# Seven landing places for the down projection's units, and three small moves ahead of the first gate

## The reference, cut to what matters

```python
h = _rms(x, g_mix); z = h @ w_in
za, zu, zv, zq, zg = jnp.split(z, SPLITS, axis=-1)
ya = gelu(_s5(za, ...))                                  # diagonal state space model
ya = (ya * sigmoid(ya @ w_glu + b_glu)) @ w_a_out
yb = _sgu(zu, zv, ...) @ w_b_out                         # gelu(zu) * (w_s @ layernorm(gelu(zv)) + b_s)
yc = _mem_xattn(zq, mem, g_mem, w_kv) @ w_c_out          # 4 heads, 256 memory rows
gates = sigmoid(zg + b_gate)                             # three gates of 1024
x = x + (gates0 * ya + gates1 * yb + gates2 * yc) @ w_out
hf = _rms(x, g_ffn)
x = x + (silu(hf @ w_gate) * (hf @ w_up)) @ w_down       # hidden width 2816
return _rms(x, g_final)
```

## Time and profile before

| | |
|---|---|
| median of 3 runs | 777.63 us (777.61 to 778.03) |
| the profiled execution's own time | 777.84 us |
| its span, first to last instruction | 776.1 us |
| TensorE busy | 765.6 us, 99% |
| VectorE busy | 541.6 us, 70% |
| ScalarE busy | 354.3 us, 46% |
| POOL busy | 315.8 us, 41% |
| granted TensorE clock, mean | 0.999 |

### The profile page before, as it was taken

One profiled execution on the slowest core, in us unless ns is written; L12 is line 12 of the kernel. 1 busy time (PEld: TensorE's weight loads), 2 busy tenths in 40 slices (PEclk: granted clock), 3 DMA queues, 4 the chain that ended last, 5 costly groups with the idle time before them and its releaser, 6 DMA issues.

```text
span 776.1 us, 9751 instructions
## 1 busy us (share of the span) xinstructions
PE 765.6 (99%) x3576; PEld 630.8 (81%) x3576; DVE 541.6 (70%) x729; ACT 354.3 (46%) x526; POOL 315.8 (41%) x169
## 2 busy tenths in 40 slices
PE   9999999999999999999999999999999999999996
PEld 7778887788888888888888888888888888778885
DVE  6999997684848484345865677777776777635686
ACT  6896567644545434543433333332323233444463
POOL 4456646233333333444444344534444453920000
PEclk9999999999999999999999999999999999999999
DMA  7744332132222432232324465666756557677852
GB/s 274 297 142 135 110 109 86 31 102 82 82 82 82 132 139 82 82 108 84 106 96 146 147 206 180 214 230 203 228 186 196 204 200 246 196 246 249 280 179 109
DMA packets 39667, 121.98 MB, mean 157 GB/s; under 512 B 4048, under 2 KB 4176, under 8 KB 37840
## 3 DMA queue, kind: packets, MB, share of 16 engines
q1 hardware_dynamic: 39488, 121.26, 47.1%
q10 hardware_dynamic: 144, 0.26, 0.1%
HBM read 104.99 MB, written 16.52 MB: 157 GB/s over the span
## 4 chain that ended last, share of the span: by engine, by line
PE 78%; DVE 13%; ACT 3%; issue 2%; DMA 2%; POOL 1%; SPq 0%; POOLq 0%; DVEq 0%; ACTq 0%
PE bank L1557 21%; PE bank L1558 21%; PE bank L1559 21%; PE bank L1926 4%; PE bank L1928 4%; PE bank L1927 4%; DVE pow_tmp L969 3%; DVE tab_tmp L969 1%; DVE s5p L969 1%; PE bank L1798 1%; DMA xT<-xt_dram 1%; DMA raw<-mix_dram 1%; DVE m_lo L974 1%; ACT prob L655 1%; DVE h_lo L974 0%
## 5 line engine op out<-in xcount | busy, mean ns | idle before, releaser
L500 POOL TENSOR_TENSOR w_lo<-raw,w_hi 128x1024 fp32r<-128x1024 f32 x90 | 219.1, 2434 | 298.1 <-ACT w_hi L561 298.1
L561 ACT ACTIVATE w_hi<-raw 128x1024 fp32r<-128x1024 f32 x112 | 118.6, 1060 | 309.1 <-PE bank L1559 302.3
L1557 PE MATMUL bank<-h_hi,w_hi 128*128 128x512 f32 x608 | 238.2, 392 | 0.5 <-DVE th L969 0.4
L1559 PE MATMUL bank<-h_hi,w_lo 128*128 128x512 f32 x608 | 236.7, 389 | 0.0
L1558 PE MATMUL bank<-h_lo,w_hi 128*128 128x512 f32 x608 | 236.6, 389 | 0.0
L1557 PEld LDWEIGHTS bank<-h_hi,w_hi 128*128 128x128 f32 x608 | 114.1, 188 | 25.5 <-DVE th L969 1.3
L1559 PEld LDWEIGHTS bank<-h_hi,w_lo 128*128 128x128 f32 x608 | 114.1, 188 | 23.9
L1558 PEld LDWEIGHTS bank<-h_lo,w_hi 128*128 128x128 f32 x608 | 114.2, 188 | 23.3 <-issue 0.2
L505 POOL TENSOR_TENSOR w_lo<-raw,w_hi 128x512 fp32r<-128x512 f32 x48 | 67.2, 1422 | 56.3 <-ACT w_hi L561 49.7
L969 DVE TENSOR_TENSOR mix<-mix 128x512 f32<-128x512 f32 x44 | 47.2, 1072 | 10.5 <-DMA mix<-w_dram 9.4
L969 DVE TENSOR_TENSOR lo<-raw,hi 128x1536 fp32r<-128x1536 f32 (+1 forms) x19 | 33.3, 1757 | 28.8 <-ACT hi L888 28.8
(11 more groups left out here) (297 smaller groups left out, 1391.7 us busy)
## 6 DMA issues: line engine op xcount, KB each, us to landing
raw<-w_dram SPq DMA_DIRECT2D x112, 512.0 KB, 3.4
mix<-w_dram SPq DMA_DIRECT2D x11, 1024.0 KB, 7.7
mix_dram<-mix SPq DMA_DIRECT2D x11, 1024.0 KB, 6.4
raw<-w_dram SPq DMA_DIRECT2D x32, 256.0 KB, 3.9
raw<-mix_dram SPq DMA_DIRECT2D x28, 256.0 KB, 3.9
half_dram<-odd SPq DMA_DIRECT2D x11, 256.0 KB, 7.9
second<-half_dram SPq DMA_DIRECT2D x3, 768.0 KB, 6.0
raw<-mix_dram SPq DMA_DIRECT2D x3, 768.0 KB, 4.3
```

The lines of the kernel that those rows point to most:

```text
L500: nc.gpsimd.tensor_tensor(w_lo[:, s, :], raw[:, s, :], fv(w_hi[:, s, :]), ALU.subtract).then_inc(w_ready, 1)
L561: nc.scalar.activation(w_hi[:, slot, :], raw[:, slot, :], ACT.Copy).then_inc(w_rounded, 1)
L1557: mm(out, a[0], b[0], start=first, stop=False)
L1559: return mm(out, a[1], b[0], start=False, stop=last)
```

## The change: what it does

Four things. (1) The units get seven raw places instead of five, a third one behind the first two `raw_d` and one where `mix` had its second half; `UNIT_SLOT` and the waits of `load_unit` follow, unit 10 is loaded ahead of the first of three, and ScalarE's first rounding of three waits for one more split. (2) The first gate waits for three groups of the gating unit instead of four, and the gate in bank 1 for the fourth. (3) ScalarE rounds tile T_VU+6 ahead of the scaling of head 2. (4) VectorE makes the memory's diagonal ahead of the products with the state space model's input matrix.

```diff
-        raw_d = [at(f"raw_d{i}", o_h + 12288 + 4096 * i, [P, TILE]) for i in range(2)]
-        unit_raw = [raw[:, 0, :], raw[:, 1, :], raw_c[:, :], raw_d[0][:, :], raw_d[1][:, :]]
-        UNIT_SLOT = (0, 1, 2, 3, 4, 0, 1, 2, 0, 1, 2)
+        raw_d = [at(f"raw_d{i}", o_h + 12288 + 4096 * i, [P, TILE]) for i in range(3)]
+        raw_e = at("raw_e", o_e + 12288, [P, TILE])
+        unit_raw = [raw[:, 0, :], raw[:, 1, :], raw_c[:, :], *(r[:, :] for r in raw_d), raw_e[:, :]]
+        UNIT_SLOT = (0, 1, 2, 3, 4, 5, 6, 0, 1, 2, 6)
...
-        unit_loaded = [sem(f"unit_loaded{i}") for i in range(5)]
+        unit_loaded = [sem(f"unit_loaded{i}") for i in range(7)]
...
                 if k < 2:
                     sp.wait_ge(w_ready, T_DN - 1 + k)
-                elif 3 <= k < 5:
+                elif 3 <= k < 6:
                     sp.wait_ge(w_used, T_DN)
-                elif k >= 5:
-                    unit_split(sp, {5: 0, 6: 1, 7: 2, 8: 5, 9: 6, 10: 7}[k])
+                elif k == 6:
+                    sp.wait_ge(mix_stored, 16 * PAIRS)
+                elif k > 6:
+                    unit_split(sp, {7: 0, 8: 1, 9: 2, 10: 6}[k])
...
-            for k in range(6, 10):
+            for k in range(6, PAIRS):
                 load_unit(k)
             load_three(0)
-            load_unit(10)
             load_three(1)
...
             round_weights(T_VU + 5)
+            round_weights(T_VU + 6)
             softmax_scale(2)
             gelu_u(1)
-            round_weights(T_VU + 6)
             round_weights(T_VU + 7)
...
                 if u == 0:
-                    act.wait_ge(w_ready, T_DN + 5)
+                    act.wait_ge(w_ready, T_DN + 6)
...
                 low_tile(norms["m"], m_hi, m_lo, memf, C_GMEM, k)
 
+            token_scale(2, 2, mtstd[:, :], mtrstd[:, :], mdiag[:, :, :], diag_m)
+
             bre, bim, cre, cim = (grid(c0) for c0 in (C_BRE, C_BIM, C_CRE, C_CIM))
...
             link(tt(bpow[1][:, L - 1, :, :], bb_tmp[:, 2, :, :], bb_tmp[:, 3, :, :], ALU.add))
-            token_scale(2, 2, mtstd[:, :], mtrstd[:, :], mdiag[:, :, :], diag_m)
-
...
-            pe.wait_ge(sgu_taken, 4)
+            pe.wait_ge(sgu_taken, 3)
             pe.wait_ge(pt_act, 4)
...
                 def gate(j, b, free):
                     if free > 0:
                         pe.wait_ge(j1_g, free)
+                    elif b == 1:
+                        pe.wait_ge(sgu_taken, 4)
```

## The result

The changed kernel takes 779.4 us against 777.65 for the kernel before, measured beside it on the same chip. The ratio is 1.0025, with a 95% interval of 1.0017 to 1.0033. It is slower by a quarter of a per cent: less than 2 us, but the interval does not take in 1. The forecast was 777.8, and its range ended at 779.1. The profiled execution took 779.2 us, with a span of 777.5 where it was 776.1 before: +1.4. The medians in this document are of the undisturbed executions; the profiled one of the run that has the rounding alone was disturbed (959.48 us at a mean clock of 0.753), so no timeline of that kernel is read.

What follows compares the result with a forecast made beforehand. TensorE was taken as the bound, busy 765.6 of 776.1 us, so only waits could move. +1.9 up to the first gate and -1.7 for the places gave +0.2: 778.0 profiled, 777.8 as median; range 775.2 to 779.1.

Steps and rivals of the forecast that it cites:

- The diagonal: Memory's diagonal made earlier on VectorE: TensorE's wait at 47.38 goes, 0.42 to 0.5 gained, 0.2 carried to the scores at 102.
- The rounding's chain of collisions: Before the first gate: T_VU+6 rounded early makes POOL and VectorE meet twice on their port; value rows late, 2.4 lost.
- the second collision: POOL's whole-tile split of T_J1 against VectorE's short scaling and last two table sums: VectorE waits some 2.0.
- The values product itself: First values product on TensorE, waiting for the value rows: starts at 132.2 instead of 129.81, 2.4 lost.
- The gate: First gate, asking for three groups instead of four: TensorE's wait there goes, 0.5 gained once.
- Seven places: Down projection: units 7 to 10 load earlier, waits at units 9 and 10 go, 1.7 gained (late end 1.2).
- Rival 1: Before the first gate: the collisions don't come; 774.5, or 775.6 with the second collision alone; chance 0.19.
- Rival 2: Down projection: added loads delay units 3 and 4, costing 1.4 to 3.6, total 779.2 to 781.4; chance 0.10.
- POOL's backlog: Down projection, in rival 2: POOL's waiting work hides 0.8 of the delay of unit loads.

## Why the prediction was wrong, step by step

**The diagonal.** Right as to its wait: none stands at its product. The two traces are 0.39 apart at the scores at 102, twice the 0.2 that was carried, but the start of this product differs by more than that among the traces of these kernels for other reasons (46.62 to 48.21), so the size is not secured. With the gate's edit it is worth 0.9 between the medians of the places alone and of all but the rounding, for 0.7 in the sum.

**The rounding's chain of collisions.** Right in mechanism and nearly in size. The prediction left open which engine takes the port first at 113.6; it was VectorE, so `srec` was on time and the table products behind it were late (3.44 for two of 1.2). T_VU+6 was rounded at 112.19 (predicted 112.6), u's third tile was taken by 124.21 (123.53 + 0.68; predicted 124.3 to 124.8), T_J1 was rounded at 124.78, the whole tile's split held a short scaling for 2.09, and the values product started at 131.96 (predicted 132.2). This term was +2.4 and measured +2.15. The run with T_J1 rounded late, which takes only the second collision away, has the values product at 129.73, where it was 129.81 before: the second collision is what made it late, and the first ate what the edit was to gain.

**The values product itself.** This is the step that failed. "The first values product starts at 132.2 instead of 129.81: 2.4 lost" took for granted that all behind the start keeps its length. The prediction gave TensorE a wait of 3.6 us (132.2 less 128.6), in a kernel in which it otherwise hardly stops, and priced only the wait: the slower clock behind it stood in no term of the sum. The four matmuls behind it ran at the lower clock: 3.34 for 1.72, **1.6 more**. The run with the wait filled took 1.5 of that away (1.82 for 3.34) and left the rows as late as they were, and it landed at 777.62, on the forecast of 777.8. Nothing shown of the kernel before had such a wait at this place, so no row priced what follows one.

**The gate.** Right: no wait there. It gave back 0.69 where 0.5 was put down. So the predicted +1.9 up to the gate was +3.08: the 1.6 above, less 0.25 by which the values product was earlier than said, less 0.2 here.

**Seven places.** Right: from the gate to the first of three 1.56 in the trace, and 1.72 from unit 5's start on (3.24 late there, 1.52 at the first of three); 1.9 between medians, for 1.7. The wait ahead of unit 5 stayed, as said.

**Rival 1** (no collisions, 774.5 to 775.6) did not happen, though the runs that took the second collision or the early rounding away landed on 775.56 and 775.07, within its bounds; neither is just the case that it priced. **Rival 2** (loads in each other's way) cost at most 0.2 of its 1.4 to 3.6: unit 3's data kept ScalarE waiting 1.1 longer, and 0.2 of that reached TensorE, near what the prediction's 0.8 for POOL's backlog leaves over. That the added loads are the cause isn't shown. With the places alone ScalarE waited 3.42 there, TensorE's start at unit 3 is not late, and the run gained 1.9.

With the missing term the sum would have been +0.2 + 1.6 = +1.8, which is 779.4 on the median shown. That it meets the median to 0.1 is in part luck. The trace's own terms, 2.15 + 1.62 - 0.69 - 1.56 - 0.1, give 1.4, and the 1.6 is the price in one execution, which by the mean clocks is hardly the same in all.

## What to carry to other kernels

Price a new wait of the matrix engine twice: the wait, and the slower clock of what stands behind it if the wait is long (3.36 us cost 1.6 more here; 1.68, 1.49 and 1.16 left the clock at 1.00 and cost 0.1 more). No run here has a wait between 1.68 and 3.36, so where the clock begins to fall is open. Before moving an instruction of one engine earlier, follow everything that it releases earlier on the engine that shares a port with VectorE, two tiles on, since the damage here was done by the tile after the next. And where an order can't be freed of a collision, put what the bottleneck waits for ahead of it; but check what then slides into the next one, as the table sums did.

## What the runs showed of the hardware

The clock's fall in a wait could be kept off with useless work: fourteen small products of ones in a wait of 3.4 us made the kernel 1.8 us faster. POOL's subtraction of a whole tile held VectorE's work between places in SBUF until the subtraction ended, however small the held instruction: 2.09 for a scaling of 128 x 2 that takes 0.17, and 3.37 for a sum that takes 1.21, of which 1.07 lie behind the subtraction's end. The value rows, whose source is in PSUM, were not held: 1.40 at 130.51 beside a split that began at 130.58, as in the kernel before. Where VectorE came first, POOL's subtractions were the ones that grew: 3.40 for a whole tile that takes 2.40, and 4.03 for two halves at 119.03, behind VectorE's product at 118.99. Two halves that VectorE did not hold up, in the run with all but the rounding, took:

```profile
110.81 2.56 POOL L507 TENSOR_TENSOR w_lo<-raw,w_hi 128x512 fp32r<-128x512 f32 x2 [3.78 <-ACT w_hi L563]
```

The Trainium skill, "SBUF — State Buffer", section "SBUF: two separate sides", calls this an exclusive lock; the trace agrees, with VectorE's scaling ending at 128.32 and POOL's split at 128.30.
